# Turning scan blocks on another engine, a fourth weight buffer and all closing gathers at once, in a one-layer hybrid step

## The reference

```
tmat = triangular_solve(eye + lmat, eye)          # per head, direction, chunk
u, w = tmat @ v_beta, tmat @ (k_beta * exp(g))
v_new = u - w @ S
o = q_dec @ S + intra @ v_new
S = S * exp(g_last) + k_dec^T @ v_new
```

## Time and profile before

| | before |
|---|---|
| median of 3 runs | 2504.52 us (2502.2 to 2506.75) |
| profiled execution, its own time | 2506.25 us |
| profiled execution, span | 2504.3 us |
| granted TensorE clock, mean | 0.928 |
| busy: TensorE | 2159.4 us, 86% |
| busy: VectorE, ScalarE, GpSimd | 906.5, 682.8, 266.2 us |
| moved by DMA | 210.12 MB in 240544 packets |

### The profile page before, as it was taken

The page is one execution under the profiler, slowest core; times in us unless marked ns, Lnnn a source line. Parts: engine busy times, 40 slices in busy tenths (PEclk is TensorE's granted clock), DMA queues, the critical chain, the costliest instruction groups (busy, mean ns, idle before and its releaser), DMA issues. The chain is left out here.

```text
span 2504.3 us, 39485 instructions
## 1 busy us (share of the span) xinstructions
PE 2159.4 (86%) x16431; PEld 1329.9 (53%) x16431; DVE 906.5 (36%) x1760; ACT 682.8 (27%) x1386; POOL 266.2 (11%) x381
## 2 busy tenths in 40 slices
PE   4987999989997587888897999999999699799960
PEld 3545676665553477877753555555455444344420
DVE  3254666634883355455551011010223300000116
ACT  6122666643441232332220000000111122122223
POOL 2000000000000444433100000000000000000013
PEclk8998999999998698999898999999999699999985
DMA  9324000010100232323203111120313455776225
GB/s 331 130 88 121 4 4 1 2 43 26 30 0 1 43 63 46 62 43 58 57 0 92 26 34 43 25 67 1 136 60 117 150 185 179 250 239 214 85 101 201
DMA packets 240544, 210.12 MB, mean 84 GB/s; under 512 B 130348, under 2 KB 202352, under 8 KB 239728
## 3 DMA queue, kind: packets, MB, share of 16 engines
q1 hardware_dynamic: 223632, 152.93, 20.5%
q0 software_dynamic: 11696, 36.31, 4.9%
q10 hardware_dynamic: 5040, 18.35, 1.8%
HBM read 165.37 MB, written 42.01 MB: 83 GB/s over the span
## 5 line engine op out<-in xcount | busy, mean ns | idle before, releaser
L741 PE MATMUL ps<-R 128*128 128x512 f32 (+1 forms) x816 | 301.2, 530 | 11.3 <-SPq L525 8.4
L1008 PE MATMUL ps<-R 128*128 128x512 f32 (+1 forms) x768 | 286.1, 526 | 19.9 <-DMA R<-in_w_dn_br_dram 17.8
L1084 PE MATMUL ps<-R 128*128 x560 | 260.1, 619 | 25.7 <-SPq L653 22.5
L900 PE MATMUL ps<-R 64*64 64x64 f32 x5120 | 181.7, 230 | 67.8 <-ACT R L1280 30.5
L741 PEld LDWEIGHTS ps<-R 128*128 128x128 f32 x816 | 158.6, 195 | 150.7 <-issue 132.8
L1008 PEld LDWEIGHTS ps<-R 128*128 128x128 f32 x768 | 147.2, 192 | 152.3 <-issue 144.9
L900 PEld LDWEIGHTS ps<-R 64*64 64x64 f32 x5120 | 172.0, 145 | 87.4 <-ACT R L1280 37.4
L1084 PEld LDWEIGHTS ps<-R 128*128 128x128 f32 x560 | 110.7, 199 | 169.6 <-issue 169.6
L1753 DVE TENSOR_TENSOR R<-ps,R 128x512 f32<-128x512 f32 (+1 forms) x48 | 28.9, 603 | 394.1 <-ACT R L1353 393.3
L1920 DVE COPY R<-ps 128x256 f32<-128x256 f32 x35 | 14.9, 425 | 383.4 <-PE ps L1109 383.4
L2071 POOL DMA_INDIRECT R<-h_scratch,slot_i x35 | 33.0, 942 | 1124.6 <-DVE slot_i L1903 749.6
(11 more groups left out here) (265 smaller groups left out, 2700.0 us busy)
## 6 DMA issues: line engine op xcount, KB each, us to landing
R<-in_w_mod_dram SPq DMA_DIRECT2D x12, 2048.0 KB, 9.1
slot_output<-R ACTq DMA_DIRECT2D x35, 512.0 KB, 3.6
R<-in_w_gate_e_dram SPq DMA_DIRECT2D x16, 1024.0 KB, 6.8
R<-in_w_up_e_dram SPq DMA_DIRECT2D x16, 1024.0 KB, 10.2
R<-in_w_down_e_dram SPq DMA_DIRECT2D x16, 1024.0 KB, 12.0
R<-in_w_in_dram SPq DMA_DIRECT2D x30, 512.0 KB, 5.4
R<-tu_scratch SPq DMA_DIRECT2D x160, 64.0 KB, 2.6
R<-in_x_sample_dram SPq DMA_DIRECT2D x16, 512.0 KB, 6.0
```

What stands on the lines that cost most here:

```text
L741: last = mm(ps[:, u % 4, 0:w], w_sb[n % NW][:, k, :], hT[:, k, c0:c0 + w], start=(k == 0), stop=(k == KD - 1))
L900: last = mm(ps[lo, bank, a * C:(a + 1) * C], lhs(a)[lo], rhs(a)[lo], start=start and (alone or a == 0), stop=stop and (alone or a == PAIRS ...
L1008: mm(ps[:, o + x, 0:w], wk[:, x, k, :], hT[:, k, c0:c0 + w], start=(k == 0), stop=(k == KD - 1))
L1084: last = mm(ps[:, 2 + t % 2, :], hsT[t % 2][:, k, :], R[:, bass.ds(at + (RB + k * 512), 512)], start=(k == 0), stop=(k == KD - 1))
```

## The change

Four things change. In the scan, `b_turn`, and the inverse in its two layouts (`b_t`, `b_u`), are made on VectorE, each by a multiplication with a mask of 0 and 1 by partition (`block_dir`, two new constant columns, which tell the directions apart) and a multiply-and-add of the transposed reading; ScalarE's two copies are gone. Its transfers cover both directions, and on the way from and to the blocks both steps, at once: GpSimd's four stores of a step become two, SP's four loads of blocks for two steps one, its eight stores two and its sixteen loads eight, with the same bytes. The store of the context's state comes after the inverses of base 4. Expert weights have four places (`RING_AT`), the fourth in memory that the router stage uses; so the fourth load goes out once the tables are ready. The router of tile 8 is issued ahead of the turning of tile 9. All 20 gathers of the closing stage go to places of their own and are issued in a row, with one semaphore for two tiles; GpSimd gates tiles 5 to 9 and VectorE tiles 0 to 4.

The core of the diff (semaphore increments and waits within an engine left out where they don't matter):

```diff
-RING_E = 3
+RING_AT = (0, 6144, 12288, 20992)
+RING_E = len(RING_AT)
...
+    parts = [...] + [eye, -eye, rot, before, (part[:, None] // 16) % 2 == np.arange(2)[None, :]]
...
-        hsT = [h2T[i] for i in range(2)]
+        hsT = [R3[:, 6144 + i * D:7168 + i * D].rearrange("p (k t) -> p k t", k=KD) for i in range(2)]
-        yg = [R3[:, i * D:(i + 1) * D] for i in range(2 * NY)]
+        yg = [R4[:, i * D:(i + 1) * D] for i in range(10)] + [R3[:, i * D:(i + 1) * D] for i in range(10)]
+        GATED = range(5, NT)
@@ SP, scan
+        def planes_of(x, n, h):
+            return bass.AP(x.tensor, (16 * n + 8 * h) * PLANE, [[C, C], [PLANE, 8], [1, C]])
+        def blocks_of(x, n):
+            return bass.AP(x.tensor, 16 * n * PLANE, [[16 * C + 16, P], [C, 16], [1, 16]])
             def inverses_back(b):
                 sp.wait_ge(S["base_done"], b + 1)
-                sp.wait_ge(S["base_turned"], b + 1)
                 for s in (2 * b, 2 * b + 1):
                     if s - 4 >= 0:
-                        sp.wait_ge(S[f"tu_in{(s - 4) % 3}"], landed(s - 4, 3, 8))
-                    for d in range(2):
-                        for x in range(2):
-                            src = b_inv if x == d else b_invt
-                            sp.dma_start(blocks_of(tu_d, 2 * (s % 4) + x, d), src[block_rows(s, d)]).then_inc(S["tu_out"], 16)
-                sp.wait_ge(S["tu_out"], 128 * (b + 1))
+                        sp.wait_ge(S[f"tu_in{(s - 4) % 3}"], landed(s - 4, 3, 4))
+                for x, src in enumerate((b_t, b_u)):
+                    sp.dma_start(blocks_of(tu_d, 4 * x + 2 * (b % 2)), src).then_inc(S["tu_out"], 16)
+                sp.wait_ge(S["tu_out"], 32 * (b + 1))
                 for s in (2 * b, 2 * b + 1):
                     if s - 2 > 0:
                         sp.wait_ge(S["vn_mm"], s - 2)
                     for x in range(2):
-                        for d in range(2):
-                            for h in range(2):
-                                sp.dma_start(tu[s % 3][h * C:(h + 1) * C, x, 4 * d:4 * d + 4], planes_of(tu_d, 2 * (s % 4) + x, d, h)).then_inc(S[f"tu_in{s % 3}"], 16)
-            for s in range(NCK):
-                sp.wait_ge(S["lt_out"], 64 * (s + 1))
-                if s % 2 == 0 and s > 0:
-                    inverses_back(s // 2 - 1)
-                if s // 2 > 0:
-                    sp.wait_ge(S["base_done"], s // 2)
-                    sp.wait_ge(S["bt_turned"], s // 2)
-                for d in range(2):
-                    sp.dma_start((b_turn, b_in)[d][block_rows(s, d)], blocks_of(lt_d, s, d)).then_inc(S["bt_in"], 16)
-                if s == CTX_CH + 2:
+                        for h in range(2):
+                            sp.dma_start(tu[s % 3][h * C:(h + 1) * C, x], planes_of(tu_d, 4 * x + s % 4, h)).then_inc(S[f"tu_in{s % 3}"], 16)
+            for b in range(NCK // 2):
+                sp.wait_ge(S["lt_out"], 64 * (b + 1))
+                if b > 0:
+                    sp.wait_ge(S["base_done"], b)
+                sp.dma_start(b_in, blocks_of(lt_d, 2 * b)).then_inc(S["bt_in"], 16)
+                inverses_back(b)
+                if b == CTX_CH:
...
-            inverses_back(NCK // 2 - 1)
@@ SP, experts
-            for e in range(2, RING_E):
-                expert_load(e)
+            expert_load(2)
             sp.wait_ge(S["dve_once"], 9)
+            for n in (NT - 2, NT - 1):
+                sp.wait_ge(S[f"h2_out{n % 2}"], landed(n, 2))
+            expert_load(3)
@@ TensorE
+                if n == NT:
+                    router(n - 2)
                 if 1 <= n <= NT:
                     h2_turned(n - 1)
-                if n >= 2:
+                if n >= 2 and n != NT:
                     router(n - 2)
@@ ScalarE, scan (both removed; even steps only)
-                    f(b_turn[C:2 * C].rearrange("p r c -> p c r"), b_in[C:2 * C], ACT.Copy).then_inc(S["bt_turned"], 1)
...
-                    f(b_invt.rearrange("p r c -> p c r"), b_inv, ACT.Copy).then_inc(S["base_turned"], 1)
@@ VectorE, base(b, first, end)
                 if first == 1:
...
+                    dve.wait_ge(S["bt_in"], 16 * (b + 1))
+                    v.tensor_scalar(b_turn, b_in, block_dir[:, 0:1], None, ALU.mult)
+                    v.scalar_tensor_tensor(b_turn, b_in.rearrange("p r c -> p c r"), block_dir[:, 1:2], b_turn, ALU.mult, ALU.add)
                 for i in range(first, end):
                     substitute(b, i)
+                if end == 16:
+                    if b > 0:
+                        dve.wait_ge(S["tu_out"], 32 * b)
+                    for x, dst in enumerate((b_t, b_u)):
+                        v.tensor_scalar(dst, b_inv, block_dir[:, x:x + 1], None, ALU.mult)
+                        v.scalar_tensor_tensor(dst, b_inv.rearrange("p r c -> p c r"), block_dir[:, 1 - x:2 - x], dst, ALU.mult, ALU.add)
@@ GpSimd, scan
-                    for d in range(2):
-                        for h in range(2):
-                            pool.dma_start(planes_of(lt_d, n - 1, d, h), la[(n - 1) % RING][h * C:(h + 1) * C, 1, 4 * d:4 * d + 4]).then_inc(S["lt_out"], 16)
+                    for h in range(2):
+                        pool.dma_start(planes_of(lt_d, n - 1, h), la[(n - 1) % RING][h * C:(h + 1) * C, 1]).then_inc(S["lt_out"], 16)
@@ closing stage: ScalarE waits for tiles in pairs, VectorE gates tiles 0 to 4, GpSimd the others
-                    act.wait_ge(S[f"y_in{n % NY}"], landed(n, NY, 2))
+                    act.wait_ge(S[f"y_in{n // 2}"], 64)
-                    if n % 2 == 1:
+                    if n not in GATED:
                         v.tensor_tensor(y0, y0, gate_rows[:, 0 if n < 2 else 1, :], ALU.mult)
-            for n in range(NY):
-                tokens_back(n)
             for n in range(NT):
-                if n % 2 == 0:
...
-                if n + NY < NT:
-                    tokens_back(n + NY)
+                for k in range(2):
+                    pool.indirect_dma_start(yg[2 * n + k], None, y_d, bass.IndirectOffsetOnAxis(ap=pos_i[:, k, n:n + 1], axis=0)
+                                            ).then_inc(S[f"y_in{n // 2}"], 16)
+            for n in GATED:
+                pool.wait_ge(S["summed"], n + 1)
+                g.tensor_tensor(yg[2 * n], yg[2 * n], gate_rows[:, 0 if n < 2 else 1, :], ALU.mult).then_inc(S["gated"], 1)
```

More of the change, by code:

```diff
@@ L68, in shape_constants @@
     before = (part[:, None] < free[None, :]).astype(np.float32)
-    parts = [np.eye(P), same, np.ones((P, P))] + upto + after_bd + level + [eye, -eye, rot, before]
+    parts = [np.eye(P), same, np.ones((P, P))] + upto + after_bd + level + [eye, -eye, rot, before, (part[:, None] // 16) % 2 == np.arange(2)[None, :]]
     return np.concatenate([np.asarray(a, np.float32) for a in parts], axis=1)
 def small_constants():
-    step = [e % RING_E for e in range(NE)]
+    at = [RING_AT[e % RING_E] for e in range(NE)]
     rows = [np.arange(T // SLOTS) * float(SLOTS), np.arange(HT), (np.arange(NE)[None, :] < np.arange(NE)[:, None]).ravel(),
-            [6144.0 * (step[e + 1] - step[e]) if e + 1 < NE else 0.0 for e in range(NE)], 128.0 * np.arange(MT + 1), np.arange(P) - 128.0, [4, 3, 2, 1]]
+            [float(at[e + 1] - at[e]) if e + 1 < NE else 0.0 for e in range(NE)], 128.0 * np.arange(MT + 1), np.arange(P) - 128.0, [4, 3, 2, 1]]
     row = np.concatenate([np.asarray(r, np.float32) for r in rows])
@@ L129, in build @@
         levels = take(2 * 2 * C).rearrange("p (l d c) -> p l d c", l=2, d=2)
-        eye_st, neg_eye, rot, before = take(C), take(C), take(P), take(P)
+        eye_st, neg_eye, rot, before, block_dir = take(C), take(C), take(P), take(P), take(2)
         small = sb("small", [P, small_np.shape[1]])
@@ L336, in build @@
         kd, qd, kdec, rv = [by_head(scr(512, "R1")) for _ in range(4)]
-        b_in, b_turn, b_inv, b_invt = [scr(256, "R1").rearrange("p (r c) -> p r c", r=16) for _ in range(4)]
+        b_in, b_turn, b_inv, b_u = [scr(256, "R1").rearrange("p (r c) -> p r c", r=16) for _ in range(4)]
+        b_t = b_in
         b_tmp = scr(256, "R1")
@@ L402, in build @@
         EW = 6144
-        ew = [R[:, RB + i * EW:RB + (i + 1) * EW] for i in range(RING_E)]
+        ew = [R[:, RB + o:RB + o + EW] for o in RING_AT]
         hs = [R3[:, 8192 + i * D:8192 + (i + 1) * D] for i in range(2)]
-        hsT = [h2T[i] for i in range(2)]
+        hsT = [R3[:, 6144 + i * D:7168 + i * D].rearrange("p (k t) -> p k t", k=KD) for i in range(2)]
         hid = [R3[:, 10240 + i * 256:10240 + (i + 1) * 256] for i in range(2)]
@@ L1290, in _ @@
                     f(growth[n % RING], bank8(1), ACT.Exp).then_inc(S["gr_ready"], 1)
-                if n >= 2 and n % 2 == 0 and n // 2 - 1 < NCK // 2:
-                    b = n // 2 - 1
-                    act.wait_ge(S["bt_in"], 64 * (b + 1))
-                    if b > 0:
-                        act.wait_ge(S["base_done"], b)
```

(26 more changed lines are left out.)

52 lines of the change are left out of this document (21 added, 31 removed).

## The result

The changed kernel takes 2482.35 us (median of five, 2480.75 to 2489.43), the kernel before 2502.87 on the same chip: a ratio of 0.9919, 95% interval 0.9904 to 0.9934. The forecast was 2481. It had been worked out from three executions of the kernel before with a median of 2504.52, as a gain of 24.5 us; between the two medians here the gain is 20.5. The hit on the time itself is thus in part luck: the kernel before came out 1.65 us faster this time, and the 2481 had been rounded up by 1. The profiled execution took 2483.34 us, with a span of 2481.4, 22.9 us shorter than before's 2504.3.

A forecast was written before the change was run, and what follows sets the result against it. TensorE's waits in the scan (94 us idle) and a closing stage largely waiting on its three-tile ring were the room. Scan 13.3 + router 3 - load 2 + closing 10.2 = 24.5 off 2504.52 gave 2480.0, stated as 2481; range 2466 to 2497.

The forecast's parts named there:

- Closing: Closing stage: early gathers make VectorE the bound, each GpSimd gate holds it about 1.77 us; gain 10.2 us, bounds 7.3 to 19.
- Rival C: Closing stage: GpSimd's gates hold nobody, so the kernel takes 2472 us; chance 0.13.
- Ring of four: Expert stage: a fourth weight buffer leaves SP's order and TensorE's six waits of 22.5 us as they are; 0 us.
- Rival E: Expert stage: the ring of four does take the six waits away, 22.5 us less, 2458 us; chance 0.04.
- The fourth load: Before the experts: the added 3 MB load, issued with the first slot gather, delays it; loss 0 to 3.6 us, 2 taken.
- Router: Before the last turning: tile 8's router fills TensorE's idle time; gain 2.4 us, 4.6 if the clock stays up, 3 taken.
- Scan: DeltaNet scan: fewer transfers and turning on VectorE together gain 13.3 us, bounds -4 and 22.
- Rival B: Scan gives nothing, as VectorE's turning takes back what the transfers free; 2493.3 us, chance 0.22.
- D: Scan gains 20 us or more, for want of holding of VectorE; 2474 us, chance 0.11.
- F: Scan: turning at both ends of the base costs a pair over 6 us, not 3.8; slower, 2510 us; chance 0.05.
- the filling gets 1.9 shorter: Start of the scan: filling the pipeline, its longest wait for the inverses at 8.3 us, gets 1.9 us shorter.
- 5.3 given back: Scan: when TensorE comes earlier it waits for the mask instead, which takes 5.3 us back over the pairs.

The follow-up runs named there:

- gates_vector: Changed kernel with all ten gates of the closing stage on VectorE, none on GpSimd: 2482.23 us, ratio 0.9916 to the kernel before.
- gates_alternate: Changed kernel with GpSimd gating tiles 0, 2, 4, 6 and 8, all 20 gathers still issued first: 2495.1 us, ratio 0.9966 to the kernel before.
- three_buffers: Changed kernel with three expert buffers instead of four and no fourth load before the first expert: 2477.69 us, ratio 0.9905 to the kernel before.
- two_behind: Changed kernel, ring of four, each load waiting for the expert two back instead of the one just before: 2448.19 us, ratio 0.9796 to the kernel before.
- fourth_later: Changed kernel with the fourth expert's load issued after the first gather has landed: 2480.55 us, ratio 0.9914 to the kernel before.
- gpsimd_later: Changed kernel with GpSimd's product of the scan's odd steps held until the turning behind the base ends: 2474.76 us, ratio 0.9898 to the kernel before.
- transfers_split: Changed kernel, turning still on VectorE, the scan's other transfers split in two or four again: 2513.93 us, ratio 1.0053 to the kernel before.

## Why the prediction was right

- **Closing, 10.2 forecast, 10.2 measured.** A tile takes 5.36 us with its gate on VectorE and 5.87 with it on GpSimd, where 5.34 and 5.84 were taken from the earlier trace rows. The operation beside each GpSimd gate takes 3.05 or 3.06 us in all five tiles. gates_vector shows the holding, gates_alternate that the split is what makes the early gathers pay. Rival C falls. The Trainium skill ("SBUF — State Buffer", on the shared port pair) states that a VectorE instruction with two SBUF inputs and a GpSimd instruction that reads SBUF exclude each other for a whole instruction; the trace agrees, with the 3.05 or 3.06 us of all five tiles. Moving these gates to VectorE had been put at 2.5 us from the rows, and gates_vector gives 2.6.
- **Ring of four, 0 forecast.** The waits went from 22.5 us in six to 21.4 in six, and three_buffers has 21.0. They are SP's order, as argued, and two_behind shows it: with that order changed they vanish. Rival E was impossible with this loop.
- **The fourth load, +2 forecast, +3.7 measured.** The mechanism holds (three_buffers, fourth_later); the size was at the bound of 3.6, since the gather meets the whole load. A middle value was a poor choice there: the load's issue at the gather's moment was known.
- **Router, 3 forecast, 2.8 to 3.1 measured.** One router fills the wait (2.69 us left of 4.48), and the other still runs at the lower clock, 3.60 us for 16 products, against 3.65 for 32 just before. The other bound, a clock that stays up, didn't come; it was added up wrong too, as 2.4 and half of 3.4 make 4.1, not 4.6. The forecast doesn't hang on it.
- **Scan, 13.3 forecast, 11.6 measured**, 10.8 with the median of the unedited scans, and some 7.5 with like fills compared. The signs and the holding are right, the size was too high, and that the profile came within 1.7 us of it owes to the short fill and is luck. On the way back from a base the first load goes out 1037.25 - 1032.32 = 4.93 us behind the first store, and eight loads are issued in 6.71 us, so four in 3.4; taken were 5 and 3. The eight waits for inverses vanished as forecast. The held turning was sized at 6.3 us; gpsimd_later takes 5.4 out of the scan behind the fill, 3.7 of it in waits for the mask. Turning behind the base was taken at 2.1 and is 0.35 + 0.64 twice with gaps, 2.1. The matmuls behind the fill are busy 312.3 us instead of 316.4 (313.1 is the median of the seven): 4.0 were forecast. Rival B falls, since all seven unedited scans are shorter than before behind the fill; transfers_split shows that VectorE's turning does take back more than half of what the transfers free, 15 of 26 us. D falls as holding is there. F falls too: the six turning operations of a pair take 0.38 + 0.68 and 2 x (0.62 + 0.70), 3.7 us, where 1.05 + 2.1 + 0.7 were taken.
- **What failed in the scan's sum are two terms: "the filling gets 1.9 shorter" and "5.3 given back".** Compared with the two fills like its own, that of the kernel before was only 0.8 to 0.9 us longer. At the mask, the working comes to 29.8 + 14.9 - 6.8 + 5.3 + 1.2 + 6.3 = 50.7 us of waits, and 54.2 are there: 3.5 off, so 8.8 were given back if the other terms were sized right. In all, TensorE idles 4.1 us less than before behind the fill, where the terms of the forecast make 7.4.

Two things stay open. TensorE's work in the fill takes 27.1 us in four of the fourteen profiles and 22.9 to 23.9 in the other ten; what decides which isn't shown. And behind the fill the same code still takes 368.7 to 374.8 us, so with one profile of the kernel before, the scan's gain is known to a few us only.

## What to carry to other kernels

When a change moves work from one engine to another and shrinks transfers at once, cost each half by itself: here they were +15 and -26 us, and there was more to gain in the first half (the mask ahead of the turning, 12 us). A deeper ring helps only if its owner's waits let it: read what the counter comes behind, not only how many buffers there are; here one index in a wait was worth 34 us, and the fourth buffer without it cost 4. Before a difference of a few us is put down to a change, look at how far the same stretch differs between profiles of the same code: the fill of this scan took 54.9 or 58.5 us with nothing changed, the router's stretch 43.6 to 43.8. And a large transfer that has time should not be issued at the moment a small one on the path goes out.

## What the runs showed of the hardware

- A wait of TensorE costs more than its length, and the granted clock is lower where there are more of them. Behind the 3.85 us wait, 64 matmuls take 3.60 us instead of 2.08. Doing the turning twice put 21 us of work on the path and took 27; removing 21.4 us of waits from the expert stage gave 33.7, with the same 1182 matmul records busy 402.72 us instead of 415.44.
- The price of an issue on SP's queue grows far more slowly than the transfer: a load took 0.617 us in the median for 64 KB (160 of them) and 0.635 for 128 KB (80), a store 0.490 for 32 KB and 0.612 for 128 KB (20). On GpSimd's queue four stores of 64 KB took 2.54 us, two of 128 KB 1.41.
- The same instructions can run at either clock level from one run to the next. Early in the scan four products took 2.04 or 2.05 us in four profiles and 1.10 in the other ten, and with the same scan code the fill was 58.5 or 58.6 us in two profiles with the first and 54.8 to 55.9 in five with the second.
- A gather of 128 rows that goes out together with a 3 MB load is waited for 3.7 us longer (9.3 against 5.6 in three_buffers).
- A product of 1.3 us on GpSimd holds VectorE's scalar multiply beside it as well (0.82 us against 0.35), an operation that reads one tile and one column.
